# Feed-forward inputs by two lanes at a time on alternating PSUM banks, in a two-layer trunk kernel

## What is computed

```python
def swiglu_ffn(h, w_in, w_out):
    gate, up = jnp.split(h @ w_in, 2, axis=-1)
    return (jax.nn.silu(gate) * up) @ w_out

for i in range(2):
    x = x + 0.5 * swiglu_ffn(rmsnorm(x, ffn1_norm[i]), ffn1_w_in[i], ffn1_w_out[i])
    ...
    x = x + 0.5 * swiglu_ffn(rmsnorm(x, ffn2_norm[i]), ffn2_w_in[i], ffn2_w_out[i])
return rmsnorm(x, final_norm)
```

## Time and profile before

| | us |
|---|---|
| three timed runs, median (lowest to highest) | 2358.85 (2358.15 to 2359.25) |
| the profiled execution | 2361.74 |
| its span, first to last instruction | 2360.0 |
| TensorE busy in it | 2338.9 |
| `ffn_in` phases, first to last matmul start | 112.18 to 353.93, 865.32 to 1105.35, 1225.26 to 1469.26, 1988.77 to 2228.80 |

### The profile page before, as it was taken

How to read it: one execution, slowest core, us unless ns; L and a number is a source line. 1 busy time by engine, 2 the same in 40 slices (tenths; PEclk the granted TensorE clock), 3 DMA queues, 4 the chain that set the end, 5 groups by cost and what they waited for, 6 DMA issues and landing times.

```text
span 2360.0 us, 29512 instructions
## 1 busy us (share of the span) xinstructions
PE 2338.9 (99%) x10944; PEld 1943.8 (82%) x10944; DVE 1202.3 (51%) x1419; ACT 747.3 (32%) x1013; POOL 263.5 (11%) x236
## 2 busy tenths in 40 slices
PE   9999999999999999999999999999999999999998
PEld 9988888877888888888878888887788888888887
DVE  6654443456888654444445444344337644444422
ACT  4432222234445322222223223123333322322322
POOL 3400001111333320000110000110001212000000
PEclk9999999999999999999999999999999999999999
DMA  7733333332222333333333333333232233333322
GB/s 231 217 92 95 98 98 96 93 107 62 80 71 75 104 93 95 97 98 98 98 89 93 95 97 98 98 98 98 71 93 87 85 95 106 98 98 95 93 94 93
DMA packets 400691, 234.32 MB, mean 99 GB/s; under 512 B 7692, under 2 KB 386672, under 8 KB 400624
## 3 DMA queue, kind: packets, MB, share of 16 engines
q1 hardware_dynamic: 397328, 223.37, 32.0%
q0 software_dynamic: 3280, 10.02, 1.2%
q10 hardware_dynamic: 16, 0.00, 0.0%
HBM read 227.07 MB, written 6.29 MB: 99 GB/s over the span
## 4 chain that ended last, share of the span: by engine, by line
PE 91%; DVE 4%; ACT 1%; issue 1%; POOL 1%; DMA 0%; DVEq 0%; ACTq 0%; SPq 0%; POOLq 0%
PE acc L1031 25%; PE acc L1033 25%; PE acc L1032 25%; PE acc L786 1%; PE acc L785 1%; PE acc L784 1%; PE mix L407 1%; PE mix L394 1%; DVE w_lo L1193 1%; PE acc L258 1%; PE acc L260 1%; PE acc L259 1%; PE mix L260 1%; PE mix L258 1%; PE mix L259 1%
## 5 line engine op out<-in xcount | busy, mean ns | idle before, releaser
L1193 DVE TENSOR_TENSOR w_lo<-raw,w_hi 128x1024 fp32r<-128x1024 f32 (+1 forms) x422 | 545.7, 1295 | 653.7 <-ACT w_hi L1464 642.8
L1031 PE MATMUL acc<-h_hi,w_hi 128*128 128x512 f32 x1920 | 757.3, 394 | 7.6 <-DVE h_lo L1256 5.4
L1033 PE MATMUL acc<-h_hi,w_lo 128*128 128x512 f32 x1920 | 748.6, 390 | 0.0
L1032 PE MATMUL acc<-h_lo,w_hi 128*128 128x512 f32 x1920 | 748.3, 390 | 0.0
L1464 ACT ACTIVATE w_hi<-raw 128x1024 fp32r<-128x1024 f32 (+1 forms) x422 | 436.5, 1038 | 354.7 <-DMA raw<-in_ffn_w_out_dram 221.8
L1031 PEld LDWEIGHTS acc<-h_hi,w_hi 128*128 128x128 f32 x1920 | 361.5, 188 | 84.5 <-DVE h_lo L1256 6.6
L1032 PEld LDWEIGHTS acc<-h_lo,w_hi 128*128 128x128 f32 x1920 | 361.5, 188 | 75.7 <-issue 2.2
L1033 PEld LDWEIGHTS acc<-h_hi,w_lo 128*128 128x128 f32 x1920 | 361.1, 188 | 75.3
L1031 PE MATMUL acc<-act_hi,w_hi 128*128 128x512 f32 (+1 forms) x976 | 367.7, 377 | 2.8 <-DVE act_lo L1205 1.2
L1033 PE MATMUL acc<-act_hi,w_lo 128*128 128x512 f32 (+1 forms) x976 | 365.8, 375 | 0.0
L1032 PE MATMUL acc<-act_lo,w_hi 128*128 128x512 f32 (+1 forms) x976 | 365.7, 375 | 0.0
(11 more groups left out here) (219 smaller groups left out, 1788.7 us busy)
## 6 DMA issues: line engine op xcount, KB each, us to landing
raw<-in_ffn_w_in_dram SPq DMA_DIRECT2D x176, 512.0 KB, 3.7
raw<-in_ffn_w_out_dram SPq DMA_DIRECT2D x70, 512.0 KB, 4.0
raw<-in_hgrn_w_in_dram SPq DMA_DIRECT2D x40, 512.0 KB, 3.7
raw<-in_gmlp_w_in_dram SPq DMA_DIRECT2D x40, 512.0 KB, 3.7
raw<-in_mem_w_kv_dram SPq DMA_DIRECT2D x32, 512.0 KB, 4.6
raw<-in_gmlp_w_out_dram SPq DMA_DIRECT2D x24, 512.0 KB, 4.0
raw<-in_ffn_w_out_dram SPq DMA_DIRECT2D x24, 384.0 KB, 3.4
raw<-in_hgrn_w_out_dram SPq DMA_DIRECT2D x16, 512.0 KB, 4.1
```

The costliest lines, as they stand in the source:

```text
L1031: pe.matmul(bank, top[:, i, :], hi, start=(start and i == 0), stop=False)
L1032: pe.matmul(bank, top[:, i, :], lo, start=False, stop=False)
L1033: m = pe.matmul(bank, rest[:, i, :], hi, start=False, stop=(stop and i == last))
L1193: dve.tensor_tensor(lane_of(w_lo, q, j)[:, 0:nkb], lane_of(raw, q, j)[:, 0:nkb], f32(lane_of(w_hi, q, j)[:, 0:nkb]), ALU.subtract).then_in ...
```

## The change

On PE the four calls of `in_unit` in an iteration of `ffn_in` become two calls of a new function `in_pair`, for lanes 0 and 1 and for lanes 2 and 3. It waits for both banks and both lanes' `w_lo` first. Then, for each of the 8 blocks of `h`, it issues high times high of one lane and of the other, high times low of both, low times high of both, so that neighbouring matmuls write different banks. Both lanes count `unit_done` at the pair's end. In the first pair of a phase the waits for `h_lo` stand once for each block, and L1097's matmul stands behind the pair. `hgrn_in` and `gmlp_in` keep `in_unit`.

On DVE and ACT the steps of an iteration keep their number and get another order: the `lo` and `hi` of lanes 2 and 3 stand together at the head (in the first iteration ahead of `norm_stats` and `root`), then come both evictions of the first pair, then `lo` and `hi` of lanes 0 and 1 of the next quad together, then the evictions of the second pair. SP's program is the same.

```diff
@@ tensor
+            def in_pair(ph, s, it, p, first=False):
+                js, q = (2 * p, 2 * p + 1), ph.q0 + it
+                if first and s == 0:
+                    pe.wait_ge(sem("v_staged"), 4 * LANES - 3 + js[1])
+                pe.wait_ge(acc_read, ph.g0 + LANES * it + js[1] - 3)
+                pe.wait_ge(w_lo_ready, LANES * q + js[1] + 1)
+                tops, rests = [lane_of(w_hi, q, j) for j in js], [lane_of(w_lo, q, j) for j in js]
+                for k, (hi, lo) in enumerate(h_parts):
+                    if first and p == 0:
+                        pe.wait_ge(h_lo_ready, DB * s + k + 1)
+                    for a, w in zip(js, tops):
+                        pe.matmul(acc[a][:], w[:, k, :], hi, start=(k == 0), stop=False)
+                    for a, w in zip(js, tops):
+                        pe.matmul(acc[a][:], w[:, k, :], lo, start=False, stop=False)
+                    for a, w in zip(js, rests):
+                        m = pe.matmul(acc[a][:], w[:, k, :], hi, start=False, stop=(k == DB - 1))
+                        if k == DB - 1:
+                            m.then_inc(unit_done, 1)
+                if first and p == 0:
+                    pe.wait_ge(sq_sum_ready, DB * (s + 1))
+                    pe.matmul(mix[3][:], ones[:], sq_sum, start=True, stop=True).then_inc(ss_done, 1)
...
-                        for j in range(LANES):
-                            in_unit(ph, s, it, j, first)
+                        for p in range(LANES // 2):
+                            in_pair(ph, s, it, p, first)
@@ vector
                         lo(ph.q0 + it, 2)
+                        lo(ph.q0 + it, 3)
                         if first:
                             norm_stats(s)
                         gate(0)
-                        lo(ph.q0 + it, 3)
                         up(1)
+                        rest(1)
                         lo(ph.q0 + it + 1, 0)
-                        rest(1)
+                        lo(ph.q0 + it + 1, 1)
                         gate(2)
-                        lo(ph.q0 + it + 1, 1)
                         up(3)
                         rest(3)
@@ scalar
                         hi(ph.q0 + it, 2)
+                        hi(ph.q0 + it, 3)
                         if first:
                             root(s)
                         silu(0)
-                        hi(ph.q0 + it, 3)
                         top(1)
                         hi(ph.q0 + it + 1, 0)
+                        hi(ph.q0 + it + 1, 1)
                         silu(2)
-                        hi(ph.q0 + it + 1, 1)
                         top(3)
```

## The result

| | before, us | changed, us |
|---|---|---|
| median of 12 runs each (lowest to highest) | 2359.2 (2358.15 to 2361.57) | 2364.7 (2362.71 to 2365.54) |
| span of the profiled execution | 2360.0 | 2363.8 |

The ratio is 1.0021 with a 95% interval from 1.0013 to 1.0028, so 3.1 to 6.6 us slower. The forecast was +3.9 us. One of the four runs of the kernel before with nine extra copies (experiment 10) took 2922.11 us at a granted clock of 0.752, the other three 2374.10 to 2375.34; it is left out of that kernel's time and ratio.

What follows compares the result with a forecast made beforehand. TensorE's matmul issue, one every 0.2266 us, was taken as the bound. The terms 0+0+(1.15+1.18)+1.6 gave +3.9 us on 2358.85, so 2362.8 us, range 2359 to 2369.

Steps and rivals of the forecast that it cites:

- Part 1: Feed-forward input loops: alternating banks at every matmul changes the pitch by 0, within 4 us in all either way.
- (b): Input loops: a bank switch at every matmul costs something; at 2 ns a switch 2371 us; chance 0.04.
- (c): Input loops: alternation shortens the pitch of 0.2266 us, giving 41 us, 2322 us; chance 0.04.
- (d): Input loops: alternation brings clock falls in some iterations; one per stage costs 7 us, 2370 us; chance 0.02.
- Part 2: Steady input loop: paired weight loads and evictions stay hidden, cost 0, with 2.7 us of slack.
- (a): Steady input loop: the second lane's load lands late in every iteration, about 88 us, 2451 us; chance 0.05.
- Part 3: Input stage starts: first matmul also awaits lane 1's `w_lo`; net +1.15 in stage 1, +1.18 in stage 3, otherwise 0.
- Part 4: Each input stage's third pair: the norm one unit later delays `w_lo`, 0.4 us a stage, 1.6 in all.
- (e): Stage starts: idle times only trade places and the clock stays up, within 1 us of now, 2359; chance 0.05.
- the clock term of stage 1: Stage 1 start: the low-clock stretch lies partly over longer idle time, losing 1.1 us instead of 1.7.

Runs made afterwards that it cites:

- experiment 10: Kernel before with nine extra unused copies on ScalarE in each loop iteration, ahead of the next lane 0's `w_hi`: 2374.22 us, ratio 1.0067.
- experiment 2: Changed kernel with pairs and joint waits kept, but one lane's 24 matmuls issued before the other's: 2365.83 us, ratio 1.0029.
- experiments 7 and 9: Changed kernel with extra unused copies on ScalarE in each loop iteration: seven in the former, 2365.95 us; nine in the latter, 2415.1 us.
- experiment 3: Changed kernel with the norm's product issued inside the first pair, behind its fifth block, instead of behind the pair: 2364.43 us, ratio 1.0022.
- experiment 1: Changed kernel with the first two units of each feed-forward input stage issued one after the other as before: 2358.86 us, ratio 0.9998.
- experiments 4 to 6: experiment 4, experiment 5 and a third kernel, which extends the latter's split and order to the HGRN and gMLP input stages: 2350.19 us, ratio 0.9959.
- experiment 5: Kernel before with split first two units, lane 3's `w_hi` and `w_lo` ahead of the norm, norm's product ahead of unit 0's last blocks: 2356.2 us.
- experiment 4: Kernel before, no pairs, with the first two units of each feed-forward input stage split, blocks 0 to 5 of both first: 2362.18 us, ratio 1.0015.

## Why the prediction was right

The forecast was 2362.8 us with a range from 2359 to 2369; 2364.7 was measured. By its steps:

- Part 1, banks, 0: measured 0 (0.22667 us from start to start before, after and without alternation, experiment 2). Rivals (b), (c) and (d) are out: no pitch changed in either direction, and the clock shows no fall inside the loops. The prediction's 0.2259 and 0.2264 us came from counts that include matmuls begun before the window; by their start times the final half of the kernel before ran at 0.22667 as well (2293.058 to 2352.218, 261 distances), so its conclusion stands firmer than its figures. The Trainium skill's page "TensorE: Matmul & The Clock Gate" tells in its section "A second HAM failure mode: psum-queue depth-cycling" of a kernel that cycled through banks, was idle for short times between groups of matmuls and lost its clock by that. This kernel switches bank at every matmul, without idle time, at a clock of 1.00: the change of bank alone doesn't bring the falls. That page's section "Back-to-back issue gap" gives about 216 ns as the gap between single matmuls of 512 columns at the full clock. That isn't reached in any order here; these fp32r products stay at 227.
- Part 2, steady loop, 0 with 2.7 us of room: measured 0 with 2.8, and experiments 7 and 9 put the end of the room at seven copies. Rival (a) is out. (Its price was 0.3 us an iteration too low by its own numbers: a landing of 10.5 against the 8 allowed is 2.5 over, not 2.2.)
- Part 3, stage 1: +1.75 of idle time forecast, +1.75 measured. The term beside it was wrong: -0.6 because a fixed stretch of low clock would lie partly over idle time. The fall came 1.4 us later than in the trace of before and lay wholly over work, so this part was 0. Stage 3: +3.43 and -2.25 forecast; measured are 3.25 more gap and 1.88 less length, the latter being the lost wait less Part 4's cost. The first matmul follows `w_lo` by 0.11 us there, where 0.26 was reckoned. The falls of the clock stayed in both stages, so rival (e) is out. Stages 2 and 4: hidden, as forecast with 0.09 us to spare.
- Part 4: 0.4 in each stage; measured 0.42 and 0.44 in the two stages that have nothing else, and gone in experiment 3.
- Sum: 3.9 forecast, 4.4 in the traces; the missing half microsecond is the clock term of stage 1, 0.6, less the 0.2 that stage 3 came sooner. The medians are 5.5 us apart, 1.1 more than the stages of the two traces. Each trace is one execution: that of the kernel before took 2361.74 us, 2.5 above its median, that of the changed kernel 2365.54, 0.8 above its own. In 28 executions of the kernel before on another chip the span went with the granted clock, 2358.7 us on average at 0.997, 2357.3 at 0.998 and 2355.7 at 0.999. So the time lost to falls differs from one execution to the next, and a share of the 5.5 us may be that; how large it is no run shows.

The forecast drew the line of what can be told from no change at 0.2% and gave most chance, 0.59, to a result within it. The measured 0.21% lies at that line, with an interval that reaches to both sides of it but leaves no change out: the measurement told more than I had allowed for, and the time is longer, to which I had given 0.37.

What stays open is when a given idle time makes the clock fall. In stage 1 2.3 to 2.4 us of idle time brought a fall in the kernel before, alone and with seven and nine copies, and in experiment 1, and none in experiments 4 to 6. The moment doesn't sort them: with 2.27 us idle the kernel before with nine copies starts the stage at 110.49 us and has the fall, experiment 5 at 111.04 and has none. In the HGRN input the same 2.21 us brought a fall in the kernel before and none in experiments 4 and 7, and the 2.09 us in stage 3 brought none with nine copies. The same 4.0 us ahead of stage 1 brought one stretch in the changed kernel and about two in experiments 3 and 9. The cause is not shown.

## What to carry to other kernels

Where a loop's matmuls start at an even pitch with no gap, as here, a new order within it changes nothing but the room that is left; look for its cost where the loop is entered, since a joint wait for two lanes turns the later lane's preparation into a wait there. When a result that others need (here the norm's sum) moves later, list what stands behind its consumer in each engine's program, not only who waits for it: what was overlooked in this way cost 1.7 us of idle time and 1.9 to 2.0 us in all in each stage of experiment 4. And the cheap gain in such a kernel was the race at the stage starts: issuing the blocks of two units whose inputs are ready, and the late blocks after them, gave 0.4% at all six input stages, falls of the clock included.

## What the runs showed of the hardware

Changing the PSUM bank at each matmul, and the stationary block at each, left the start-to-start time of a 128x512 fp32r product at 0.22667 us, over 911 distances in a row. A fall of the clock lasts some 3.4 us at 1.2 GHz and cost up to 1.7 us each time in these traces. The same place in the program, with the same idle time before it, had none or one in different kernels (2.27 us ahead of stage 1, 2.21 us in the HGRN input), or one or two (4.0 us ahead of stage 1), which is as large as the effects that were being measured: below 2 us a difference has to be read by stage, not from the total.
